# Two feed-forwards of a ten-stage network on one core: high weights meet 288 and 256 columns in place of 272 and 272

## The reference, cut to what matters

```
def rmsnorm(x, g):
    xf = x.astype(jnp.float32)
    y = xf * lax.rsqrt(jnp.mean(xf * xf, axis=-1, keepdims=True) + NORM_EPS)
    return (y * g.astype(jnp.float32)).astype(x.dtype)

def swiglu(x, w_gate, w_up, w_down):
    return (jax.nn.silu(x @ w_gate) * (x @ w_up)) @ w_down
...
for l in range(DEPTH):
    h = h + 0.5 * swiglu(rmsnorm(h, ffn1_norm[l]), ffn1_w_gate[l], ffn1_w_up[l], ffn1_w_down[l])
    h = h + hybrid_mixer(...)
    h = h + 0.5 * swiglu(rmsnorm(h, ffn2_norm[l]), ffn2_w_gate[l], ffn2_w_up[l], ffn2_w_down[l])
```

## Time and profile before

| | us |
|---|---|
| runs of before | 2168.33, 2168.32, 2167.05 |
| their median | 2168.32 |
| the profiled execution | 2168.25 |
| its span, first to last instruction | 2166.5 |
| TensorE matmul busy in it | 2159.2 |
| VectorE busy | 1473.7 |
| ScalarE busy | 1209.1 |
| GpSimd busy | 286.3 |

### The profile page before, as it was taken

One profiled execution on the slowest core, in us unless ns is written; L12 is line 12 of the kernel. 1 busy time (PEld: TensorE's weight loads), 2 busy tenths in 40 slices (PEclk: granted clock), 3 DMA queues, 4 the chain that ended last, 5 costly groups with the idle time before them and its releaser, 6 DMA issues.

```text
span 2166.5 us, 48341 instructions
## 1 busy us (share of the span) xinstructions
PE 2159.2 (100%) x18139; PEld 2140.1 (99%) x18139; DVE 1473.7 (68%) x2249; ACT 1209.1 (56%) x1759; POOL 286.3 (13%) x327
## 2 busy tenths in 40 slices
PE   9999999999999999999999999999999999999999
PEld 9999999999999999999999999999999999999999
DVE  7655997665566579886657657976656656686663
ACT  6444886544444368855555547865455535565552
POOL 0001661100100136220020011010010010102000
PEclk9999999999999999999999999999999999999999
DMA  7554435556455544455656655356655655455663
GB/s 239 178 193 163 160 126 169 173 174 199 155 180 187 181 165 143 141 191 192 206 178 194 201 187 169 124 178 194 213 170 198 211 176 180 157 170 183 193 218 130
DMA packets 100977, 386.57 MB, mean 178 GB/s; under 512 B 11376, under 2 KB 12528, under 8 KB 100880
## 3 DMA queue, kind: packets, MB, share of 16 engines
q1 hardware_dynamic: 100368, 383.95, 54.3%
q0 software_dynamic: 368, 1.26, 0.2%
q10 hardware_dynamic: 144, 0.05, 0.0%
HBM read 384.18 MB, written 1.05 MB: 178 GB/s over the span
## 4 chain that ended last, share of the span: by engine, by line
PE 91%; DVE 6%; ACT 1%; issue 0%; DMA 0%; SPq 0%; ACTq 0%; DVEq 0%
PE bank L437 28%; PE bank L444 28%; PE bank L445 28%; DVE wlo L460 2%; DVE bank L1797 1%; PE bank L1105 1%; PE bank L1107 1%; PE bank L1106 1%; PE bank L1152 0%; PE bank L813 0%; ACT whi L453 0%; DVE proj L1783 0%; PE bank L996 0%; PE bank L999 0%; PE bank L998 0%
## 5 line engine op out<-in xcount | busy, mean ns | idle before, releaser
L437 PE MATMUL bank<-u,whi 128*128 128x256 f32 (+2 forms) x3776 | 1063.6, 282 | 1.9 <-DVE u L513 1.8
L444 PE MATMUL bank<-u,whi 128*128 128x256 f32 (+1 forms) x3776 | 1060.4, 281 | 0.0
L445 PE MATMUL bank<-u,wlo 128*128 128x256 f32 (+1 forms) x3776 | 1059.1, 280 | 0.0
L460 DVE TENSOR_TENSOR wlo<-raw,whi 128x1024 fp32r<-128x1024 f32 (+1 forms) x673 | 888.0, 1321 | 178.9 <-ACT whi L453 178.4
L453 ACT ACTIVATE whi<-raw 128x1024 fp32r<-128x1024 f32 (+1 forms) x673 | 741.5, 1114 | 196.3 <-PE bank L445 177.1
L437 PEld LDWEIGHTS bank<-u,whi 128*128 128x128 f32 x3776 | 710.3, 188 | 3.8 <-DVE wlo L473 1.6
L444 PEld LDWEIGHTS bank<-u,whi 128*128 128x128 f32 x3776 | 710.2, 188 | 1.0 <-issue 0.2
L445 PEld LDWEIGHTS bank<-u,wlo 128*128 128x128 f32 x3776 | 710.0, 188 | 0.0
L437 PE MATMUL bank<-hid,whi 128*128 128x256 f32 (+1 forms) x1408 | 394.2, 280 | 0.0
L444 PE MATMUL bank<-hid,whi 128*128 128x256 f32 (+1 forms) x1408 | 394.2, 280 | 0.0
L445 PE MATMUL bank<-hid,wlo 128*128 128x256 f32 (+1 forms) x1408 | 394.2, 280 | 0.0
(11 more groups left out here) (308 smaller groups left out, 2210.5 us busy)
## 6 DMA issues: line engine op xcount, KB each, us to landing
raw<-w SPq DMA_DIRECT2D x548, 512.0 KB, 3.4
raw<-w SPq DMA_DIRECT2D x128, 704.0 KB, 4.8
raw<-w SPq DMA_DIRECT2D x8, 256.0 KB, 6.0
h<-xT SPq DMA_DIRECT2D x4, 272.0 KB, 4.7
outT<-h SPq DMA_DIRECT2D x8, 128.0 KB, 4.7
consts<-cst POOLq DMA_DIRECT2D x1, 576.0 KB, 4.8
dist<-cst POOLq DMA_DIRECT2D x1, 192.0 KB, 2.7
rdist<-cst POOLq DMA_DIRECT2D x1, 192.0 KB, 3.3
```

The lines of the kernel that those rows point to most:

```text
L437: pe.matmul(out[:, cut:cols], w, x[:, cut:cols], start=first, stop=False, skip_group_check=True)
L444: pe.matmul(out, w_h, x_lo, start=False, stop=False, skip_group_check=True)
L445: return pe.matmul(out, w_l, x_hi, start=False, stop=last, skip_group_check=True)
L460: dve.tensor_tensor(weights(1, n), raw[:, n % RING, 0:COLS[n]].rearrange("p (k c) -> p k c", c=128), weights(0, n), ALU.subtract).then_inc ...
```

## The change

For phases 2 and 3 (`JOINED`) it changes four things.

1. The three matmuls of a product. The first streams 288 columns: 16 columns of the low part (the 16 meta tokens) that now lie just ahead of the high tile, and the 272 of the high tile, both with the high weights, into bank columns 0 to 287. The second streams the 256 other columns of the low part with the high weights into columns 32 to 287. The third streams 272 columns of the high part with the low weights into columns 16 to 287. So the meta tokens' low product stands in columns 0 to 15 by itself, and VectorE adds it.
2. The places. A `k`'s high and low tile lie in one piece of 640 floats (2560 bytes), the next `k` 2560 bytes on. `U_JOINED` and `HID_JOINED` set where, and `place_of` shifts the gate and up panels within their ring slots, by a table (`DISTANCES`) for each of the four slots and for high and low weights. Down panels stay at column 0.
3. VectorE's and ScalarE's instructions that follow from this: longer evacuations (288 columns against `R_long`, which holds the meta tokens' factor twice), an addition of 16 columns behind each, low parts in two pieces, the addition to `h` in three, and one more logarithm of 16 columns.
4. `R_long` is 64 floats longer than `R`, so that everything allocated behind it moves by 256 bytes, in all phases.

With the definition above the distances of phases 2 and 3 are now, per product (288, 256, 272 columns):

| panels | to their own weights | to the weights that come next |
|---|---|---|
| phase 2, gate and up | 2 or 6, 7 or 3, 3 or 7 | 2 or 6, 3 or 7, 3 or 7 |
| phase 2, down | 2, 7, 3 | 2, 7, 3 |
| phase 3, gate and up | 7 or 3, 7 or 3, 7 or 3 | 7 or 3, 6 or 2, 0 or 4 |
| phase 3, down | 6, 3, 7 | 6, 3, 7 |

The diff, cut to its core:

```
+JOINED = (2, 3)
+LONG_FIRST = {2: True, 3: True}
+U_JOINED = {2: (48, 352), 3: (16, 368)}
+HID_JOINED = {2: 8, 3: 72}
+DISTANCES = {2: ((3, 7), (3, 3), (7, 7), (7, 3)), 3: ((0, 7), (0, 3), (4, 7), (4, 3))}
+
+def place_of(part, n):
+    y = max(i for i in range(len(PHASES)) if BASE[i]["P"] <= n)
+    if y not in JOINED or COLS[n] != K8:
+        return 0
+    return 16 * ((U_JOINED[y][0] // 16 - DISTANCES[y][(n - BASE[y]["P"]) % RING][part]) % 8)
...
-        R = sb("R", [128, T])
+        R_long = sb("R_long", [128, 4 * META + T])[:, 0:META + T]
+        R = R_long[:, META:META + T]
...
         def u_at(y, part, k, c0=None, c1=T):
+            if y in JOINED:
+                at = 2 * TILE_STEP * k + U_JOINED[y][part]
+                return u[:, at + (0 if c0 is None else c0):at + c1]
...
         def hid_at(y, part, f):
+            if y in JOINED:
+                b0, at = HID_JOINED[y], (META, TILE_STEP)[part]
+                return hid[:, b0:b0 + 2 * FT * TILE_STEP].rearrange("p (k c) -> p k c", c=2 * TILE_STEP)[:, f, at:at + T]
...
-            at = META if BASE[LAST_MIX]["P"] + 20 <= n < BASE[LAST_MIX]["P"] + IN_PANELS else 0
+            at = META if BASE[LAST_MIX]["P"] + 20 <= n < BASE[LAST_MIX]["P"] + IN_PANELS else place_of(part, n)
...
+        def joined_products(pe, out, n, k, x_hi, x_lo, first, last, long_first):
+
+            w_h, w_l = weights(0, n)[:, k, :], weights(1, n)[:, k, :]
+            long, short = (out[:, 0:META + T], with_ahead(x_hi)), (out[:, 2 * META:META + T], x_lo[:, META:T])
+            for i, (o, x) in enumerate((long, short) if long_first else (short, long)):
+                pe.matmul(o, w_h, x, start=(first and i == 0), stop=False, skip_group_check=True)
+            return pe.matmul(out[:, META:META + T], w_l, x_hi, start=False, stop=last, skip_group_check=True)
...
+            if y in JOINED:
+                dve.scalar_tensor_tensor(out=ahead(u_at(y, 0, f)), in0=h[:, f, 0:META], scalar=norm_gain(y, f),
+                                         in1=u_at(y, 0, f, 0, META), op0=ALU.mult, op1=ALU.subtract)
+                dve.scalar_tensor_tensor(out=u_at(y, 1, f, META), in0=h[:, f, META:T], scalar=norm_gain(y, f),
+                                         in1=u_at(y, 0, f, META), op0=ALU.mult, op1=ALU.subtract).then_inc(u_ready, 1)
+                return
...
+                act.activation(R_long[:, 0:META], NORM[:, 0:META], ACT.Ln, bias=rms_eps)
+                act.activation(R, NORM[:, 0:T], ACT.Ln, bias=rms_eps).then_inc(log_done, 1)
+                act.wait_ge(log_done, n)
+                act.activation(R_long[:, :], R_long[:, :], ACT.Exp, scale=-0.5).then_inc(R_ready, 1)
...
-                            act.wait_ge(a_evac, g + 1 + RING * it)
+                        if y in JOINED:
+                            act.wait_ge(first_added, adds(y) + 2 * p + 1 + RING * it)
+                        else:
+                            act.wait_ge(a_evac, g + 1 + RING * it)
                         act.activation(sl[:, p, W], gt[:, p, W], ACT.Silu).then_inc(silu_done, 1)
...
+                    if y in JOINED:
+                        src = bank[4 + f % 2]
+                        dve.scalar_tensor_tensor(out=h[:, f, 0:META], in0=src[:, 0:META], scalar=factor,
+                                                 in1=h[:, f, 0:META], op0=ALU.mult, op1=ALU.add).then_inc(first_added, 1)
+                        dve.scalar_tensor_tensor(out=h[:, f, META:T], in0=src[:, 2 * META:META + T], scalar=factor,
+                                                 in1=h[:, f, META:T], op0=ALU.mult, op1=ALU.add)
+                        dve.wait_ge(first_added, adds(y) + 2 * FT + f + 1)
+                        dve.scalar_tensor_tensor(out=h[:, f, 0:META], in0=src[:, META:2 * META], scalar=factor,
+                                                 in1=h[:, f, 0:META], op0=ALU.mult, op1=ALU.add).then_inc(h_done, 1)
...
+                            dve.tensor_tensor(long[:, p, :], src[:, 0:META + T], R_long[:, :], ALU.mult).then_inc(a_evac, 1)
+                            dve.wait_ge(a_evac, g + i + 1 + it4)
+                            dve.tensor_tensor(out[:, p, 0:META], out[:, p, 0:META], long[:, p, 0:META], ALU.add)\
+                               .then_inc(first_added, 1)
...
+                        dve.tensor_tensor(ahead(hid_at(y, 0, f)), pr[:, p, 0:META], hid_at(y, 0, f)[:, 0:META], ALU.subtract)
+                        dve.tensor_tensor(hid_at(y, 1, f)[:, META:T], pr[:, p, META:T], hid_at(y, 0, f)[:, META:T],
+                                          ALU.subtract).then_inc(hid_ready, 1)
```

More of the change, by code:

```diff
@@ L400, in hid_at, with ahead, with_ahead @@
         def hid_at(y, part, f):
+            if y in JOINED:
+                b0, at = HID_JOINED[y], (META, TILE_STEP)[part]
+                return hid[:, b0:b0 + 2 * FT * TILE_STEP].rearrange("p (k c) -> p k c", c=2 * TILE_STEP)[:, f, at:at + T]
             return tile_of(hid, FT, TILE_STEP if y <= LAST_MIX else SEQ, HID_PLACE[y], y, part, f, first_col(y), T)
+        def ahead(whole):
+            return bass.AP(whole.tensor, whole.offset - META, [whole.ap[0], [1, META]])
+        def with_ahead(whole):
+            return bass.AP(whole.tensor, whole.offset - META, [whole.ap[0], [1, META + T]])
         def width(y):
@@ L484, in da_square, with adds @@
             return dqk[:, f // 2, f % 2, :] if f < 4 else (dsq if f < 6 else drq)[:, f % 2, :]
+        def adds(y):
+            return (2 * FT + KD) * JOINED.index(y)
         def norm_gain(y, f):
@@ L723, in tile @@
                                 pe.wait_ge(ready, count - (lag if K == 0 else last - K))
+                            if y in JOINED:
+                                mm = joined_products(pe, bank[4 + j % 2], n, k, x(0, K), x(1, K),
+                                                     K == 0, K == last, LONG_FIRST[y])
+                                continue
                             mm = products(pe, bank[4 + j % 2][:, 0:N], n, k, x(0, K), x(1, K),
@@ L1258, in ffn @@
                     n = b["P"] + 2 * f
-                    act.wait_ge(a_evac, b["A"] + 2 * f + 1)
+                    if y in JOINED:
+                        act.wait_ge(first_added, adds(y) + 2 * f + 1)
+                    else:
+                        act.wait_ge(a_evac, b["A"] + 2 * f + 1)
                     act.activation(sl[:, p, W], gt[:, p, W], ACT.Silu).then_inc(silu_done, 1)
@@ L1737, in tile @@
                     dve.wait_ge(silu_done, F + 1 + it2)
-                    dve.wait_ge(a_evac, g + 2 + it4)
+                    if y in JOINED:
+                        dve.wait_ge(first_added, adds(y) + 2 * (f if last else p) + 2 + it4)
+                    else:
+                        dve.wait_ge(a_evac, g + 2 + it4)
                     dve.tensor_tensor(pr[:, p, W], sl[:, p, W], up[:, p, W], ALU.mult).then_inc(prod_done, 1)
```

34 lines of the change are left out of this document (24 added, 10 removed).

## The result

The change is slower: 2171.78 us against 2167.77 (medians of 20 executions each, taken in turn on one chip), ratio 1.0019, 95% interval 1.0013 to 1.0025. That is 4.0 us more, where 4.5 less were forecast; the range held it. The profiled execution took 2171.96 us, its span is 2170.2.

A forecast was written before the change was run, and what follows sets the result against it. TensorE's stream of matmuls bounds the kernel, each costing 10.0 ns over its columns. The terms -4.6 - 0.2 + 0.3 = -4.5 us on 2168.25 gave 2163.8 us, range 2157.5 to 2173.5.

The forecast's parts named there:

- Class P: 704 products, phase 2 and phase 3's down panels: 23.4 ns over their columns instead of 30.0, -4.6 us.
- I take 6.7: The 288-column stream in phase 2 and phase 3's down panels: 6.7 ns over its columns, as with 256 columns.
- The "ends" 6.7 to 11.7: Bounds for the 288-column stream's time over its columns: lowest row 6.7 ns, first mixer's end 11.7 ns.
- rival 2: The change moves nothing: 3.3 ns more per 16 columns keeps a product 30.0 ns over its columns, 2168.6 us; chance 0.18.
- Class Q: 352 products, phase 3's gate and up panels: 29.5 ns over their columns, 0.5 ns less each, -0.2 us.
- my end of +1.8: Upper end for phase 3's gate and up panels: 35.0 ns over a product's columns, +1.8 us.
- 0.1 us at each of three boundaries: Between phases, split pieces of h and u's low part nearly fit the slack: +0.3 us, ends 0 and 1.0.
- VectorE in the panels: Longer evacuations and extra additions take 0.52 us or more per hidden tile, covered by four banks and free time: 0.
- 73 to 79%: Expected share of a gate window in which VectorE is busy, with no wait of TensorE on it.
- The move by 256 bytes: Buffers behind R_long swap distances 3 and 7 in later phases: 0, with 1.7 us either way kept for the range.
- Rival 3: New places meet worse: every product takes 375 instead of 370 ns, +5.3 us on 1056 products, 2173.9 us; chance 0.20.

The follow-up runs named there:

- the runs on the widths: The change with phase 2's addresses in both phases and one or more streams cut by 16 or more columns: 340.0 to 371.7 ns a product.
- squares on ScalarE: The change, with seven of eight squares at the first mixer's end moved from GpSimd to ScalarE: median 2169.44 us, ratio 1.0011 to the kernel before.
- both causes removed: The change with phase 2's addresses also in phase 3 and squares on ScalarE: 2167.47 us against the kernel before's 2167.74, ratio 0.9999.
- the scans: Three single executions of the change with different weight distances in each of four panels, some with other stream places or order: 370.0 to 378.8 ns a product.
- the first four experiments: The change with phase 3 alone joined (1.0008), squares on ScalarE (1.0011), phase 2's addresses in phase 3 (1.0011), even own-weight distances in phase 2 (1.0023 of the kernel before).

## Why the prediction was wrong

- **"Class P", -4.6 us: the failed step is the long stream, "I take 6.7".** It measured 13.0 ns (phase 2). The other two were off by 1.3 and -1.0: 30.0 instead of 23.4, and 0 us on 704 products. My reason, that an even number of steps ends as it begins, has no run for it; the even start, which I had priced at 11.7 at most, costs 16 on three streams of 256, and with an odd start the product of 288 is longer still. The "ends" 6.7 to 11.7 left out the true value, because I took the nearest excesses as bounds for a width that no row had. Behind the size stands the way of adding up: I gave each stream an excess of its own, and the runs on the widths show that one stream's place or width changes the steps of the others. What sets a product's excess stays open.
- **The slope of rival 2** (3.3 ns for 16 columns, 13.3 at 288, sum 30.0) gave phase 2's time exactly. It is still no law: 16 columns fewer took off 0 or 3.3 ns, or added 1.1 or 1.7.
- **"Class Q", -0.2 us:** the raised excesses were right (11.1 and 11.7 said, 11.5 and 10.8 measured), the long stream again not (6.7 said, 12.3). That is +1.6 us on 352 products, inside my end of +1.8. Phase 3's gate was the slower one, so I was wrong in size and in the rule's reach, not in which panels.
- **"0.1 us at each of three boundaries": the other failed step.** The second boundary, on which I worked it out, and the third cost nothing that shows. The first cost 2.2: there VectorE also has a split of weights in every 3.0 us, and 13.18 of 15.00 us busy stood in the earlier trace rows. I costed the pieces on the last tile only, not on the seven ahead of it, and not GpSimd beside them. With the 1.6 us of class Q this is all of the loss.
- **VectorE in the panels, 0:** right; 52.48 of 74.00 us, 71%, and no wait. My 73 to 79% was a little high by my own sum, whose lower end, 4.2 us, is 71% of 16 products at 370.0 ns. **The move by 256 bytes, 0:** right; the later phases are unchanged.
- **Rival 3** had the sign and not the mechanism: only phase 3's gate and up panels come near 375, and the larger part of the loss is a stall.

## What to carry to other kernels

Where TensorE's step is over its columns, the product of several matmuls is the unit to measure: put one product of the new widths and places on the chip and scan the places, with several executions of each, before summing excesses by stream. Where a change adds VectorE instructions, look for the stretch in which VectorE is fullest, count the whole cycle there with GpSimd's instructions that run beside it, and compare it with TensorE's cycle; a few hundredths over, repeated, end as a stall.

## What the runs showed of the hardware

**Two steps at the same places.** In the run with squares on ScalarE, phase 2 took 376.7 ns a product in every panel, though its addresses and its instructions are those of the run with both causes removed, which took 370.0:

```profile
402.00:476.00 74.00, 74.00 (x592) 74.00 (x591) 52.77 (x112) 35.27 (x49) 0.00 (x0) 1.00 0.53 172
532.00:569.00 37.00, 37.00 (x296) 37.00 (x296) 18.36 (x32) 14.71 (x15) 7.05 (x10) 1.00 0.50 164
```

Its ten executions fall into two groups, six at 2169.0 to 2169.5 and four at 2172.5 to 2173.2 us; the means differ by 3.51 us, as 528 products by 6.65 ns would. Down projections whose places no run changed came at 370.0 or 376.7 in the scans as well. The change's own 20 executions hold two at 2174.9, and 31 of the kernel before, taken with the first four experiments, one at 2172.93, with the others up to 2168.5; no trace of these three shows where. I tried whether the entry into the phase decides, by a rest of TensorE ahead of phase 2 (it waits for the eighth tile of `u` instead of the sixth; squares on ScalarE):

```
-                                pe.wait_ge(u_ready, u_base(y) + (KD - 2 if k == 0 else k + 1))
+                                pe.wait_ge(u_ready, u_base(y) + (KD if y == 2 else KD - 2 if k == 0 else k + 1))
```

> As the run with ScalarE's squares, and TensorE waits ahead of phase 2's first product for the last tile of u instead of the sixth: about 1.9 us of stall put in by hand. Theory N, how TensorE enters the phase decides between 370.0 and 376.7 ns a product, and an entry from rest gives 370.0: phase 2 at 370.0 in the profile, all executions in one group near 2171.2 (2169.3 + 1.9). Rival P, the two steps come at random in either entry: again two groups, 3.5 us apart, in a proportion like the 6 to 4 of that run.

Measured: median 2171.68 us, ratio 1.0020 (1.0011 to 1.0029), but two of ten at 2176, one of them the profiled one, with 376.7 ns throughout phase 2. N falls; an entry from rest does not give 370.0 each time. What decides between the two is open.

**No excess at 1.2 GHz.** In that profiled execution TensorE rested for 1.84 us, and the granted clock from 381 to 390 us was 0.81 on the mean, and 0.50, the 1.2 GHz level, from 386.4 to 389.1 (the change's three shorter rests in the same stretch left it at 1.00):

```profile
381.00:390.00 9.00, 7.16 (x45) 6.97 (x45) 4.70 (x10) 4.59 (x7) 1.78 (x2) 0.81 0.53 176
386.40:389.10 2.70, 2.70 (x13) 2.70 (x13) 0.76 (x1) 0.81 (x1) 0.00 (x0) 0.50 0.30 73
```

```profile
385.45 0.48 PE L489 MATMUL bank<-u,whi 128*128 128x288 f32 x2 [1.84 <-DVE u L567]
...
386.42 0.66 PE L489 MATMUL bank<-u,whi 128*128 128x288 f32 x2
...
389.14 0.58 PE L489 MATMUL bank<-u,whi 128*128 128x288 f32 x2
```

The four products from 386.42 to 389.14 us take 0.68 us each, which is 816 columns at 1.2 GHz (680.0 ns) and nothing on top. At 2.4 GHz the same product has 30 to 37 ns on top. So the excess is no fixed toll of a matmul; it appears when the columns come twice as fast, as it would if the reads from SBUF could not quite follow, though no run here shows those reads.
